# Attention of the second block: the copies and subtractions of the gate weights' split at other places of two instruction queues

## What is computed

```python
for blk in range(s // SB_BLOCK):
    z = einsum('bhqd,bhkd->bhqk', q[:, :, q0:end], k[:, :, :end]) * scale
    log_keep = where(mask, log_sigmoid(-z), 0.0)
    rest = cumsum(log_keep, axis=3, reverse=True) - log_keep
    a = where(mask, exp(log_sigmoid(z) + rest), 0.0)
    outs.append(einsum('bhqk,bhkd->bhqd', a, v[:, :, :end]))
...
gates = sigmoid(proj[..., B_Z1:G1] + b_gate)
merged = gates[..., :D] * (o_a @ w_up_a) + gates[..., D:] * (o_b @ w_up_b)
return x + merged @ w_out
```

## Time and profile before

| | |
|---|---|
| runs, us | 1444.82, 1445.28, 1448.46 |
| profiled execution, us | 1442.53 |
| its span, first to last instruction, us | 1440.8 |
| TensorE matmul busy | 1322.6 us, 92% |
| VectorE, ScalarE, GpSimd busy | 660.4, 496.3, 59.4 us |
| mean granted clock of TensorE | 0.972 of full speed |
| the attention's steps | from 1179.6 to 1261.6 us of the span |

### The profile page before, as it was taken

How to read it: one execution, slowest core, us unless ns; L and a number is a source line. 1 busy time by engine, 2 the same in 40 slices (tenths; PEclk the granted TensorE clock), 3 DMA queues, 4 the chain that set the end, 5 groups by cost and what they waited for, 6 DMA issues and landing times.

```text
span 1440.8 us, 16806 instructions
## 1 busy us (share of the span) xinstructions
PE 1322.6 (92%) x7035; PEld 1016.0 (71%) x7035; DVE 660.4 (46%) x1097; ACT 496.3 (34%) x776; POOL 59.4 (4%) x70
## 2 busy tenths in 40 slices
PE   6999999999999996788887889989989988899998
PEld 5888887678766885545554468777968875488887
DVE  4455334655466445211111168657566455413253
ACT  4334234456355423011111145354232135422231
POOL 0000000000000000112111100000000001000000
PEclk9999999999999997699999999999999999899999
DMA  6222322112222368899999952102010020112331
GB/s 226 87 86 87 117 66 81 59 59 88 88 88 88 121 239 324 345 403 403 407 401 409 371 200 88 59 0 89 1 59 1 30 88 1 59 59 88 116 117 59
DMA packets 67558, 207.41 MB, mean 144 GB/s; under 512 B 9003, under 2 KB 10141, under 8 KB 55190
## 3 DMA queue, kind: packets, MB, share of 16 engines
q1 hardware_dynamic: 61234, 192.11, 35.5%
q0 software_dynamic: 5536, 12.04, 2.8%
q10 hardware_dynamic: 708, 2.13, 0.4%
HBM read 196.33 MB, written 17.83 MB: 149 GB/s over the span
## 4 chain that ended last, share of the span: by engine, by line
PE 69%; DVE 11%; DMA 10%; ACT 6%; issue 3%; POOL 1%; SPq 0%; ACTq 0%; DVEq 0%; POOLq 0%
PE PS L543 17%; PE PS L545 16%; PE PS L544 16%; PE PS L1019 5%; DMA work<-xn_scratch,slot_tokens 4%; PE PS L540 4%; PE PS L862 3%; DMA raw<-in_w 2%; DMA scratch<-in_w 2%; PE PS L890 2%; DVE wlo L1295 2%; ACT scratch L2198 2%; ACT whi L2198 1%; ACT work L2198 1%; PE PS L707 1%
## 5 line engine op out<-in xcount | busy, mean ns | idle before, releaser
L1295 DVE TENSOR_TENSOR wlo<-raw,whi 128x2048 fp32r<-128x2048 f32 x70 | 160.3, 2291 | 270.3 <-ACT whi L2198 270.2
L2198 ACT ACTIVATE whi<-raw 128x2048 fp32r<-128x2048 f32 (+1 forms) x78 | 138.7, 1779 | 235.1 <-PE PS L545 218.4
L543 PE MATMUL PS<-whi,hthi 128*128 128x512 f32 x480 | 195.6, 407 | 5.9 <-ACT y_plain L2198 4.1
L543 PE MATMUL PS<-hthi,whi 128*128 128x512 f32 x480 | 196.6, 410 | 0.9 <-DVE htlo L1338 0.9
L545 PE MATMUL PS<-whi,htlo 128*128 128x512 f32 x480 | 188.0, 392 | 0.0
L545 PE MATMUL PS<-hthi,wlo 128*128 128x512 f32 x480 | 187.8, 391 | 0.0
L544 PE MATMUL PS<-wlo,hthi 128*128 128x512 f32 x480 | 187.7, 391 | 0.0
L544 PE MATMUL PS<-htlo,whi 128*128 128x512 f32 x480 | 187.3, 390 | 0.0
L2198 ACT ACTIVATE work<-PS 128x512 f32<-128x512 f32 (+3 forms) x148 | 81.5, 563 | 304.3 <-PE PS L890 74.2
L543 PEld LDWEIGHTS PS<-hthi,whi 128*128 128x128 f32 x480 | 90.5, 188 | 32.3 <-issue 14.2
L543 PEld LDWEIGHTS PS<-whi,hthi 128*128 128x128 f32 x480 | 90.8, 189 | 24.3 <-ACT y_plain L2198 4.3
(11 more groups left out here) (357 smaller groups left out, 1843.7 us busy)
## 6 DMA issues: line engine op xcount, KB each, us to landing
raw<-in_w_in SPq DMA_DIRECT2D x44, 1024.0 KB, 5.0
y_plain<-in_w SPq DMA_DIRECT2D x21, 1024.0 KB, 26.1
w_plain<-in_w SPq DMA_DIRECT2D x20, 1024.0 KB, 20.3
h_plain<-in_w SPq DMA_DIRECT2D x20, 1024.0 KB, 23.5
raw<-in_w SPq DMA_DIRECT2D x15, 1024.0 KB, 19.4
merged<-in_w SPq DMA_DIRECT2D x10, 1024.0 KB, 26.8
scratch<-in_w SPq DMA_DIRECT2D x10, 1024.0 KB, 27.8
raw<-in_w_gate SPq DMA_DIRECT2D x8, 1024.0 KB, 5.1
```

The costliest lines, as they stand in the source:

```text
L543: e.matmul(o, lh, rh, start=start, stop=False)
L1295: tt(lo, raw_place(j), as_f32(hi), SUB).then_inc(*ve.mark("lo", j))
L2198: return e.activation(o, i, f, bias=bias, scale=scale)
```

## The change

In VectorE's loop the piece of a turn is written one turn earlier (turns 3 to 10 instead of 4 to 11), and the clearing stands ahead of the piece, no longer behind it. In ScalarE's loop the piece is written one turn earlier too (turns 2 to 9 instead of 3 to 10), and stands ahead of the exponential and logarithm of that turn. No instruction is added or removed.

```diff
@@ vector @@
             if 0 < s < STICKS - 1:
                 stick_held(s + 1)
-            if 4 <= s < 4 + 2 * HB:
-                split_quarter((s - 4) % HB)
             if s % 3 == 1 and s // 3 + 1 < SBH // 2:
                 stick_clear(s // 3 + 1)
+            if 3 <= s < 3 + 2 * HB:
+                split_quarter((s - 3) % HB)
             if s > 3 and s % 3 == 1:
                 stick_out(s // 3 - 1)
@@ scalar @@
             if s > 3 and s % 3 == 1:
                 stick_high(s // 3 - 1)
+            if 2 <= s < 2 + 2 * HB:
+                split_quarter((s - 2) % HB)
             if s + 2 < STICKS:
                 stick_log(s + 2)
-            if 3 <= s < 3 + 2 * HB:
-                split_quarter((s - 3) % HB)
```

## The result

The changed kernel takes 1430.78 us (median of 4 runs, 1430.02 to 1433.02) against 1445.05 before (4 runs, 1444.03 to 1448.46). The ratio is 0.9907, 95% interval 0.9894 to 0.992: faster by 0.9%. The profiled execution took 1430.02 us (span 1428.3) against 1442.53, so 12.5 less.

The account below looks back on a forecast made before the run. Between attention's sums of step 3 and step 11, the copy and subtraction of pieces were taken to delay the maximum. 9.6 + 2.8 = 12.4 us off gives 1432.9 against the median (1430.1 against the profiled execution), range 1430.0 to 1439.0.

Parts of the forecast that it names:

- What bounds: Sums of step 3 to step 11: ScalarE's copy and VectorE's subtraction of a piece delay the maximum, though neither belongs to attention.
- the subtraction hides beside exponential and logarithm: VectorE's subtraction runs while ScalarE does exponential and logarithm: 0.69 against 1.72 or 2.15, with step 5 the heaviest case.
- The fit at step 5: Subtraction, clearing and out on VectorE end at 1213.94, the logarithm at 1214.07; it just fits.
- 11.78 less 2.16, so 9.6 to step 11's maximum: Waits between logarithm and maximum, steps 5 to 11, save 11.78; low parts give back 0.96 and 1.2; maximum 9.6 earlier.
- 1.00 + 7.98 + 0.8 + 0.63: From step 6's maximum to the low part behind step 8: TensorE's start, its sums, shares, high part; claimed 10.3.
- 2.8 for the clock: Step 11's sums on TensorE return from half to full clock, 6.11 to 3.30, saving 2.81.
- I take the full clock there, by the nearer row: Step 11's sums run at full clock: a 1.44 gap had left it up, and no gap above some 0.4 remains.
- The rule on short bursts: Skill page read against the clock gain: short idles between matmul bursts swing the clock; gain then nothing, change worth 9.6.
- 1432.9 against the median: Whole kernel: forecast time counted from the runs' median of 1445.28; 1430.1 against the profiled execution.
- The clock did not fall again in the stage: Rival: lower clock stays in the stage; one fall 1435.7 (chance 0.13), two falls 1438.5 (chance 0.05).
- nothing was lost behind it: Rival: gain lost behind the stage, the gates' product waiting for the next units; about 1444, chance 0.05.
- the shares did not hold up the exponentials: Part of the slower rival: shares come late, the copy ahead delays the exponential; with lower clock half the stage 1449.9, chance 0.03.

## Why the prediction was right, step by step

- **What bounds.** Right. The chain after goes from logarithm to maximum without a piece. The experiments narrow the reason: of the three moves, one turn of lead for the copy on ScalarE does all of it, ahead of the exponential or behind it. My argument that the subtraction hides beside exponential and logarithm holds, but for one step. It counted 0.69 against the logarithm everywhere but at step 5; step 8 has a clearing and an out as well, and there the fit was nil in the changed kernel and missed by 0.29 with VectorE's loop as it was (ScalarE's edit alone). The fit at step 5, counted as 0.13, was 0.14.
- **11.78 less 2.16, so 9.6 to step 11's maximum.** 9.62 measured, but that it agrees to the last digit is luck. From the start of one maximum to that of the next:

| us, steps | 4-5 | 5-6 | 6-7 | 7-8 | 8-9 | 9-10 | 10-11 |
|---|---|---|---|---|---|---|---|
| before | 6.86 | 5.60 | 4.73 | 7.07 | 5.59 | 4.93 | 6.22 |
| after | 4.30 | 5.44 | 3.61 | 4.29 | 5.83 | 3.61 | 4.30 |
| change | -2.56 | -0.16 | -1.12 | -2.78 | +0.24 | -1.32 | -1.92 |
| counted | -2.56 | -0.17 | -1.13 | -2.78 | +0.07 | -1.13 | -1.92 |

  Five steps came as counted, and two were off and cancel. From 8 to 9 the low part gives back 1.36 and not 1.2: it starts 2.49 behind the start of step 8's maximum, where it was 1.13 before (behind step 5 it is 2.09 for 1.13, so the 0.96 that was counted). The prediction's own terms for it, 1.00 + 7.98 + 0.8 + 0.63, add up to 10.4 and not to 10.3; the low part came 10.39 behind step 6's maximum. From 9 to 10 the gain is 0.19 larger than the piece's 1.13, and that part is the clock's. Rows of TensorE and of VectorE in the kernel before:

```profile
1235.33 2.97 PE L1201 MATMUL PS<-scratch,consts 128*128 128x512 f32 x4 [0.20 <-DVE scratch L2100]
1240.39 0.28 PE L1186 MATMUL PS<-mask 128*128 128x128 bf16 x2
1239.65 0.95 DVE L2100 TENSOR_TENSOR scratch<-PS,scratch 128x768 f32<-128x768 f32 x1
1240.71 0.96 DVE L2093 TENSOR_SCALAR scratch<-PS 128x768 f32<-128x768 f32 x1
```

  The lower clock lengthened step 8's sums, so step 10's scores ended at 1240.67 and the minimum came 1.06 behind step 9's maximum; behind step 6's it came after 0.86. In the second trace of the kernel before this share of the clock is 2.2 (6.92 less 4.73), and the prediction has no term for it.
- **2.8 for the clock.** 2.81 in the profiled pair, but the step "I take the full clock there, by the nearer row" rested on the gap alone. The runs leave open whether that is enough: gaps of 3.12 and 3.11 left the clock up in the changed kernel, gaps of 2.16, 3.42 and 3.62 went with a fall in the kernel before. Filling the gap does take the fall at step 11 away. What else has to come together was not settled. Nor is 2.81 a fixed sum: the sums of step 11 took 6.11 in one trace before and 4.97 in the other.
- **The rule on short bursts** ("TensorE: Matmul & The Clock Gate", section "A second HAM failure mode: psum-queue depth-cycling", in the Trainium skill) tells of short idle times between bursts that made the clock swing. The trace after does not agree: the changed stage is still made of bursts over rotating banks, with idle times of up to 0.43 between them, and its clock stays at 1.00.
- **1432.9 against the median.** 1430.78 measured. The profiled executions differ by 12.5, as counted; the medians by 14.3. The 1.8 between is within the scatter of either kernel's runs, and the kernel before has its clock's falls in it, which vary; that they make the 1.8 is not shown.
- **Rivals.** The clock did not fall again in the stage, nothing was lost behind it (179.2 in both), and the shares did not hold up the exponentials: ScalarE still waits 0.46 to 1.11 for the minimum behind each copy.

## What to carry to other kernels

When filler work is cut into pieces over two in-order queues, what counts is the lead between its two halves: if the second engine's half stands ahead of something urgent, the first engine's half must be done one turn earlier; both places for it that were tried then did. Count the gain from the start of the urgent instruction less the end of what it needs, step by step, and then look at once for the next wait in line, because here a fifth of the 11.78 went to it. Check each agreement step by step too, because errors that cancel do not show in a sum. Once the other engines no longer hold it up, TensorE's idle time in the stage is all that further moves can bring.

## What the hardware showed that was not expected

- **A subtraction beside GpSimd's additions took 1.00 us, not 0.67.** In the changed kernel the last piece's subtraction is the only one that starts well inside an addition of GpSimd. With ScalarE's edit alone, with the clearing behind the piece, and with the copies behind the logarithm three of the eight do, each 0.28 into one, and they take 0.99 to 1.00; so it is the clearing ahead of the piece that keeps the other two out. Timelines of VectorE and GpSimd in the changed kernel:

```profile
1238.80 1.00 DVE L1302 TENSOR_TENSOR wlo<-raw,whi 128x512 fp32r<-128x512 f32 x1
```

```profile
1237.83 0.73 POOL L2880 TENSOR_TENSOR merged<-scratch 128x256 f32<-128x256 f32 x1 [2.88 <-DVE scratch L2100]
1238.52 0.73 POOL L2881 TENSOR_TENSOR merged<-scratch,work 128x256 f32<-128x256 f32 x1
```

  It starts inside the second addition and ends 0.55 after it. The addition keeps its 0.73. The Trainium skill, "SBUF — State Buffer", section "Who interferes with whom", says that an instruction of VectorE with two SBUF inputs contends with one of GpSimd that reads SBUF, because its second input comes through a read interface that both share, and that the order of issue decides which of the two is blocked. The trace agrees: the later one took 0.33 longer and the earlier one did not. It cost nothing, as the logarithm was not yet there.

- **The length of the gap just before does not tell whether the clock falls.** 3.12 and 3.11 us of idle time behind a dense stretch left it at the full level in two traces. In the kernel before a gap of 2.16 us, ahead of step 9's scores, was followed by the lower level in both of its traces, within those scores in the first and behind them in the second:

```profile
1233.40 1.18 PE L1180 MATMUL PS<-y_plain 64*128 64x128 f32 x8 [2.16 <-DVE PS L2119]
1237.58 0.93 PE L1180 MATMUL PS<-y_plain 64*128 64x128 f32 x8 [2.16 <-DVE PS L2119]
```

  The gaps ahead of it in that stage had been longer (1.44 and 0.97) than in the changed kernel (0.43 at most). That this made the difference is not shown.
